# Summing the next stage's weights in quarter-width pieces beside the output product of a pooling layer

## The reference

```
x1 = x + (mix * silu(z)) @ w_out_a            # pooling layer's output, K = 2048, N = 1024
kv = rmsnorm(x1, norm_kv_g) @ w_kv            # shared keys and values
qz = rmsnorm(x1, norm_b_g) @ w_in_b           # queries and gate of the attention layer
```

## Time and profile before

| | |
|---|---|
| Time, median of 3 runs | 2968.87 us (2966.39 to 2971.01) |
| Time of the profiled execution | 2971.35 us |
| Its span, first to last instruction | 2969.7 us |
| TensorE busy | 2880.2 us, 97% |
| VectorE busy | 1802.3 us, 61% |
| ScalarE busy | 1401.6 us, 47% |
| DMA, mean over the span | 191 GB/s |
| TensorE's granted clock, mean | 0.991 of full speed |

### The profile page before, as it was taken

The page is one execution under the profiler, slowest core; times in us unless marked ns, Lnnn a source line. Parts: engine busy times, 40 slices in busy tenths (PEclk is TensorE's granted clock), DMA queues, the critical chain, the costliest instruction groups (busy, mean ns, idle before and its releaser), DMA issues. The chain is left out here.

```text
span 2969.7 us, 45966 instructions
## 1 busy us (share of the span) xinstructions
PE 2880.2 (97%) x17242; PEld 2418.4 (81%) x17242; DVE 1802.3 (61%) x2770; ACT 1401.6 (47%) x2232; POOL 128.4 (4%) x171
## 2 busy tenths in 40 slices
PE   8999999999989999999999999999999999988998
PEld 7888888888977887778888888889999999865787
DVE  3356556464443232376767666588888888644654
ACT  4444344342222222355646454377777777533322
POOL 0000000000000000000000000100000000022211
PEclk9999999999999999999999999999999999999999
DMA  7433433432526777698897878863544444399453
GB/s 254 161 116 121 155 120 116 156 123 100 197 74 216 243 247 244 230 302 288 274 300 253 274 259 252 259 159 86 114 101 111 101 110 117 131 416 405 160 187 107
DMA packets 326493, 567.27 MB, mean 191 GB/s; under 512 B 26761, under 2 KB 205561, under 8 KB 305689
## 3 DMA queue, kind: packets, MB, share of 16 engines
q1 hardware_dynamic: 324257, 564.61, 58.8%
q0 software_dynamic: 2048, 0.14, 0.0%
HBM read 424.69 MB, written 140.70 MB: 190 GB/s over the span
## 5 line engine op out<-in xcount | busy, mean ns | idle before, releaser
L2197 ACT ACTIVATE attn_scores<-attn_scores,attn_lowest 128x1024 f32<-128x1024 f32 (+15 forms) x256 | 306.7, 1202 | 2.7 <-DVE attn_lowest L2255 2.7
L2255 DVE CUSTOM_DVE_ANT_0 attn_scores<-attn_s,region_early 128x1024 f32<-128x1024 f32 (+7 forms) x256 | 216.7, 856 | 69.1 <-PE attn_s L2138 38.8
L268 PE MATMUL outa_acc<-outa_w_hi,outa_g_hi 128*128 128x512 f32 x512 | 203.9, 398 | 21.0 <-DVE outa_g_lo L1159 11.3
L268 PE MATMUL pool_acc<-pool_odd_x_hi,pool_wh 128*128 128x512 f32 (+1 forms) x640 | 223.2, 349 | 0.0
L270 PE MATMUL pool_acc<-pool_odd_x_hi,pool_wl 128*128 128x512 f32 (+1 forms) x640 | 222.9, 348 | 0.0
L269 PE MATMUL pool_acc<-pool_odd_x_lo,pool_wh 128*128 128x512 f32 (+1 forms) x640 | 222.9, 348 | 0.0
L269 PE MATMUL outa_acc<-outa_w_lo,outa_g_hi 128*128 128x512 f32 x512 | 202.2, 395 | 0.0
L270 PE MATMUL outa_acc<-outa_w_hi,outa_g_lo 128*128 128x512 f32 x512 | 201.7, 394 | 0.0
L268 PE MATMUL pool_acc<-even_x,pool_wh 128*128 128x512 f32 x512 | 200.1, 391 | 0.0
L270 PE MATMUL pool_acc<-even_x,pool_wl 128*128 128x512 f32 x512 | 199.3, 389 | 0.0
L269 PE MATMUL pool_acc<-even_x,pool_wh 128*128 128x512 f32 x512 | 199.2, 389 | 0.0
(11 more groups left out here) (364 smaller groups left out, 6962.7 us busy)
## 6 DMA issues: line engine op xcount, KB each, us to landing
region_early<-w_fold SPq DMA_DIRECT2D x110, 1024.0 KB, 6.9
pool_wz<-in_w_in_a SPq DMA_DIRECT2D x18, 2048.0 KB, 8.0
pool_wu<-w_mix SPq DMA_DIRECT2D x16, 2048.0 KB, 7.9
hold_kq<-in_cache_k SPq DMA_DIRECT2D x64, 512.0 KB, 6.9
region_early<-in_cache_v SPq DMA_DIRECT2D x60, 512.0 KB, 6.7
w_fold<-region_early SPq DMA_DIRECT2D x32, 896.0 KB, 5.6
region_early<-gatedT SPq DMA_DIRECT2D x16, 1024.0 KB, 7.8
gatedT<-pool_gates SPq DMA_DIRECT2D x48, 256.0 KB, 2.2
```

The source lines that it names most:

```text
L268: pe.matmul(out, ah, bh, start=first, stop=False)
L2197: act.activation(part, part, ACT.Exp, scale=-1.0, bias=low[s][:, x:x + 1], accum_out=sums[s][:, i:i + 1]).then_inc(expd, 1)
L2255: dve.tensor_tensor_reduce(sc[s][:, c, a0:a0 + n], s_ps[idx % 2][:, at0:at0 + n], bias[h % 2][:, b0:b0 + n], -SCALE, low[s][:, x - 2:x - 1 ...
```

## The change

Four things change. A place of an item holds 128 columns in place of 256, so that there are 64 items (`FN = 128`). They go round four slots in place of two (`NF = 4`), each with semaphores of its own. SP's load of the input rows moves from `step` to behind the items of the block (`next_x`). And on ScalarE and VectorE up to four items of a block are worked on ahead of the split (and on VectorE ahead of the add) that they followed before; the rest of the block's items stay behind it.

```diff
-        fold = [t[:, :, :].rearrange("p k n -> p (k n)")[:, 0:2048].rearrange("p (i n) -> p i n", i=8) for t in wst]
-        FN = 256
+        FN, NF = 128, 4
+        fold = [t[:, :, :].rearrange("p k n -> p (k n)")[:, h * 8 * FN:(h + 1) * 8 * FN].rearrange("p (i n) -> p i n", i=8)
+                for t in wst for h in range(2)]
...
-        fold_in, fold_out = ([m.sem(f"{n}{i}") for i in range(2)] for n in ("fold_in", "fold_out"))
+        fold_in, fold_out = ([m.sem(f"{n}{i}") for i in range(NF)] for n in ("fold_in", "fold_out"))
...
             def load_item(x):
                 kd, k, c = items[x]
                 _, w, half, _ = nxt.kinds[kd]
-                if x >= 2:
-                    sp.wait_ge(fold_out[x % 2], 16 * (x // 2))
+                if x >= NF:
+                    sp.wait_ge(fold_out[x % NF], 16 * (x // NF))
...
             def fold_items(b):
                 for x in items_of(b):
                     store_item(x)
-                    if x + 2 < len(items):
-                        load_item(x + 2)
-
-            def step(i, s, ahead, x_ahead):
+                    if x + NF < len(items):
+                        load_item(x + NF)
+
+            def step(i, s, ahead):
 
                 sp.wait_ge(added, 2 * i + s + 1)
                 dst = D["x1"][ds((2 * i + s) * P, P), :]
...
                 if ahead:
                     sp.wait_ge(g_lo, 2 * i + s + 3)
                     load_g(sp, 2 * i + s + 4, s, P)
-                if x_ahead:
-                    sp.wait_ge(out_sem[s], 16 * i + 16)
-                    load_x(2 * i + s + 2, s)
-
-            step(0, 0, True, True)
+
+            def next_x(b):
+                sp.wait_ge(out_sem[b % 2], 16 * (b // 2) + 16)
+                load_x(b + 2, b % 2)
+
+            step(0, 0, True)
             sp.wait_ge(w_lo, KC)
             sp.wait_ge(sample_mm, KC // LK)
-            load_item(0)
-            load_item(1)
-            step(0, 1, True, True)
+            for x in range(NF):
+                load_item(x)
+            next_x(0)
+            step(0, 1, True)
...
             for b in range(2, full - 2):
-                step(b // 2, b % 2, b + 4 < full, True)
+                step(b // 2, b % 2, b + 4 < full)
                 fold_items(b)
+                next_x(b)
...
             for b in range(2, full):
+                fold_items(items_of(b - 2)[:NF])
                 split(b // 2, b % 2)
-                fold_items(b - 2)
+                fold_items(items_of(b - 2)[NF:])
...
             for b in range(2, full - 2):
+                fold_items(items_of(b)[:NF])
                 add(b // 2, b % 2)
                 split(b // 2 + 1, b % 2)
-                fold_items(b)
+                fold_items(items_of(b)[NF:])
```

More of the change, by code:

```diff
@@ L1030, in load_item @@
                 _, w, half, _ = nxt.kinds[kd]
-                if x >= 2:
-                    sp.wait_ge(fold_out[x % 2], 16 * (x // 2))
+                if x >= NF:
+                    sp.wait_ge(fold_out[x % NF], 16 * (x // NF))
                 for r, at in ((k, slice(0, 8, 7)), (k + HK, slice(3, 7, 3))):
                     rows = w[r * P:(r + 1) * P, half * nxt.W:(half + 1) * nxt.W].rearrange("p (h n) -> p h n", h=2)
-                    sp.dma_start(fold[x % 2][:, at, :], rows[:, :, c * FN:(c + 1) * FN]).then_inc(fold_in[x % 2], 16)
+                    sp.dma_start(fold[x % NF][:, at, :], rows[:, :, c * FN:(c + 1) * FN]).then_inc(fold_in[x % NF], 16)
             def store_item(x):
@@ L1040, in store_item @@
                 at = k * HN + c * FN
-                sp.dma_start(D["w_fold"][kd].rearrange("i p n -> p i n")[:, :, at:at + FN], fold[x % 2][:, 0:7, :]
-                             ).then_inc(fold_out[x % 2], 16)
+                sp.dma_start(D["w_fold"][kd].rearrange("i p n -> p i n")[:, :, at:at + FN], fold[x % NF][:, 0:7, :]
+                             ).then_inc(fold_out[x % NF], 16)
             def fold_items(b):
@@ L1072, in on_sp @@
             fold_items(1)
+            next_x(1)
             for b in range(2, full - 2):
-                step(b // 2, b % 2, b + 4 < full, True)
+                step(b // 2, b % 2, b + 4 < full)
                 fold_items(b)
+                next_x(b)
                 if b == full - 4:
@@ L1080, in on_sp @@
                 sp.dma_start(first_rows[r], D["x1"][r * P:(r + 1) * P, :]).then_inc(row_sems[r], 16)
-            for s in range(2):
-                sp.wait_ge(fold_out[s], 16 * (len(items) // 2))
+            for out in fold_out:
+                sp.wait_ge(out, 16 * (len(items) // NF))
             nxt.load_raw(sp, 0)
             nxt.load_raw(sp, 1)
-            step(pairs - 1, 0, False, False)
+            step(pairs - 1, 0, False)
             sp.wait_ge(out_sem[0], 16 * pairs)
@@ L1089, in on_sp @@
             nxt.load_raw(sp, 2)
-            step(pairs - 1, 1, False, False)
+            step(pairs - 1, 1, False)
         self.mm, self.added, self.full = mm, added, full
@@ L1117, in on_act, with fold_items @@
                 act.activation(wh[:, k, :], wst[i % 2][:, r, :], ACT.Copy).then_inc(w_hi, 1)
-            def fold_items(b):
-                for x in items_of(b):
+            def fold_items(some):
+                for x in some:
                     kd, k, _ = items[x]
                     gain = gains[nxt.kinds[kd][3]]
-                    act.wait_ge(fold_in[x % 2], 32 * (x // 2) + 32)
+                    act.wait_ge(fold_in[x % NF], 32 * (x // NF) + 32)
                     for r, at in ((k, slice(0, 8, 7)), (k + HK, slice(3, 7, 3))):
-                        w = fold[x % 2][:, at, :]
+                        w = fold[x % NF][:, at, :]
                         act.activation(w, w, ACT.Copy, scale=gain[:, r:r + 1]).then_inc(fold_scaled, 1)
             for b in range(2, full):
+                fold_items(items_of(b - 2)[:NF])
                 split(b // 2, b % 2)
-                fold_items(b - 2)
+                fold_items(items_of(b - 2)[NF:])
             def row_square(r):
@@ L1175, in on_dve, with fold_items @@
                 dve.tensor_tensor(wl[:, k, :], wst[i % 2][:, r, :], f32(wh[:, k, :]), ALU.subtract).then_inc(w_lo, 1)
-            def fold_items(b):
-                for x in items_of(b):
-                    f = fold[x % 2]
+            def fold_items(some):
+                for x in some:
+                    f = fold[x % NF]
                     dve.wait_ge(fold_scaled, 2 * x + 2)
@@ L1191, in on_dve @@
             dve.tensor_tensor(xr[:, :], sample_acc[:, :], xr[:, :], ALU.add).then_inc(sample_added, 1)
-            fold_items(1)
+            fold_items(items_of(1))
             for b in range(2, full - 2):
+                fold_items(items_of(b)[:NF])
                 add(b // 2, b % 2)
                 split(b // 2 + 1, b % 2)
-                fold_items(b)
+                fold_items(items_of(b)[NF:])
             def row_average(r):
```

## The result

The changed kernel takes 3074.75 us (median of 5 runs, 3073.75 to 3079.51) against 2969.71 us before (median of 5, 2966.39 to 2973.65): a ratio of 1.0357, 95% interval 1.0344 to 1.0369, or 105 us slower. The forecast was 3111 us in a range of 3050 to 3165. The sign and the mechanism were right, the size too large by 36 us.

A forecast was written before the change was run, and what follows sets the result against it. SP's serial queue, already slower than TensorE, was taken as the bound: ten periods of 34.75 or 39.45 us put block 14's split 141.0 us later, plus 1 for clock, +142 on the median: 3111 us, range 3050 to 3165.

The forecast's parts named there:

- The bound: SP's queue in the nine blocks from 988.05: 24.4 us a block against TensorE's 22.0; shortening it earns at most some 11 us.
- n items cost n times c, whatever the slots: SP's queue: one store in the air despite four slots, 5.33 x 4.7 = 25.1 us a block against 16.8.
- The cycle c: SP's time for one item, two load issues 0.93 and a store landing 3.8: 4.7 us, range 3.8 to 5.1.
- The alternative estimate of 4.5 us: SP's time for one item, counting only what can't overlap: two load issues 0.93, then a store; some 4.5 us.
- rival 3: Fold items' DMAs: small packets run at full rate, an item takes 4.3 us, total 3092 us; chance 6%.
- The head wait: Block head: the split waits for the fourth item, loaded after the last store lands; 12.35 us, then 7.4 for g.
- The input rows: Block head: loading them behind the sums saves SP's 3.7 us x1-store wait and 0.5 MB before the first fold store.
- The clock: TensorE before the last two products: a restart after a 12 us gap at lower clock counts once, +1 us.
- The head wait is not hidden: Answers the rival that the fourth item's data come earlier: 8.55 us a block go, 94 in all, 3017 us; chance 4%.
- Small packets are cheaper than large ones: Answers the rival that 512 B store packets are no cheaper than 1 KB: 6.3 us an item, +77, 3188 us; chance 7%.
- doing nothing: Rival on the whole change: it does nothing, since the split is not late; chance 1%.
- rival 4: The change pays: SP's chain falls under 22.0 us a block and TensorE's waits go, 2956 us; chance 2%.

The follow-up runs named there:

- size_only: Kernel before with 128 columns in a place (64 items), still two slots and the old order everywhere: 3035.8 us, ratio 1.0223 to before.
- lag_no_ahead: no_ahead with SP loading item x + 3 behind the store of item x, so two stores are in the air: 2955.7 us, ratio 0.9954 to before.
- x_only: Kernel before with only the load of the input rows moved behind the items: 2972.5 us, ratio 1.0010 to before.
- no_ahead: Changed kernel with the sums behind the add and split again; small items, four slots and moved input rows stay: 3023.4 us, ratio 1.0184 to before.

## Why the prediction was right, and where its size was off

**The bound.** SP's serial chain was already slower than TensorE. Right: size_only shows it from one side, lag_no_ahead from the other, where TensorE's waits for the split vanish and 14.6 us are gained on the kernel before (the prediction's "at most some 11 us" left out the low clock behind the waits; TensorE is busy 3.9 us less).

**n items cost n times c, whatever the slots.** Right. 60 waits on the landing of the store just issued.

**The cycle c.** This is the step that was mis-sized: 4.7 us taken, 4.17 measured. The prediction had c 48 times in its sum, 48 x 0.53 = 25 us of the miss. Two numbers in it were wrong. I took 316 GB/s for small packets from a window of block loads, but the small fold stores run at 348 GB/s (first line, DMA view of the changed kernel, 1024.5 to 1025.3 us). The loads are no slower: while g is loaded, from 1013.5 to 1015.5 us, it is 346 (second line). The window of the earlier trace rows took in a slow start, 259 to 291 GB/s in its first ten slices against some 345 near its end.

```profile
DMA packets 545, 0.28 MB, mean 348 GB/s; under 512 B 1, under 2 KB 545, under 8 KB 545
DMA packets 1350, 0.69 MB, mean 346 GB/s; under 512 B 0, under 2 KB 1350, under 8 KB 1350
```

At 348 GB/s 0.72 MB are 2.07 us, which leaves 2.1 for the rest of the cycle, where I had taken 2.55 as independent of size; some of it, probably the ragged end of a store, shrinks with the item. The alternative estimate of 4.5 us, which counted only what can't overlap, was the better one, and the sum with c = 4.3 (rival 3) came nearest, at 3092 us. The Trainium skill ("DMA: Bandwidth & Descriptors", Specifications) says that 512 B is enough for line rate. The trace agrees in part: stores move 385 GB/s with 1 KB packets and 348 with 512 B, so the larger ones are 11% faster, and not the 22% that I took.

**The head wait.** Right in place and kind. Its terms, forecast and measured: last landing 3.8 and 3.35 (part of c), fourth item's loads 3.1 and 2.75, scalings 0.9 and 0.94, sums 1.05 and 0.94, add 1.2 and 1.13, split 2.3 and 2.28, g to the first landing 7.4 and 6.76. The load term makes 4 us of the miss over 11 blocks, the g term 7, sums and add 2. With 25 that is 38 us; the forecast of the median was 36 us too high, and the split of block 14 came 37.6 us earlier than forecast (1307.4 for 1345.0). TensorE's waits before blocks 4 to 14, forecast as 11 to 17 us each, are 7.1 to 12.1: SP's period is 31.6 us with five items in place of 34.75, and the product takes 23.7 us (1011.16 to 1042.86, less the wait of 8.02) in place of 22.0, at the lower clock.

**The input rows.** The claim that their gain "is real" was wrong for the reason shown in x_only: the wait was hidden behind the bytes that the same store has to follow. Between small-item kernels it is worth some 7 us in all, within the overlap of the intervals, not 3.7 a block. In the changed kernel the forecast was not hurt, since its head was summed from DMA data.

**The clock.** TensorE's lower clock after a wait, which I counted once, costs 20.6 us of busy time in all. It adds almost nothing to the end: the terms of SP's period add up to 31.6 us without one of TensorE's, so a slower product only shortens the next wait. Only behind the last wait could it count, and no run took that apart.

**The rivals.** The head wait is not hidden: without it (no_ahead) 51 us go. Small packets are cheaper than large ones, since c fell from 6.3 to 4.17. Full rate for small packets (rival 3) was nearer in c than my forecast, 4.3, but its reason holds only in part. Small items are not free, and the change is far from doing nothing. The faster case exists, at 2955.7 us where rival 4 named 2956, but by another edit: not by a shorter landing, but by not waiting for it.

## What to carry to other kernels

More buffers help only if the queue that fills them doesn't wait for the transfer it has just issued: look at what each wait names, and let it name the one before. Where a queue is serial, cutting pieces in half costs nearly the fixed part of a cycle for each new piece. Before work is put ahead of something that others wait for, ask which of its pieces arrives last, since that one sets the price; and before a wait is moved, ask which transfer the next step would wait for anyway.

## What the hardware showed that I had not expected

An instruction of SP that issues a DMA mostly takes 0.4 to 0.5 us, but the fold store's takes 5.54 to 6.32 us in ten blocks of x_only, where it stands right behind the input rows, the x1 store and g, and 3.90 to 5.04 with small items (no_ahead). This fits a queue that takes only so much before issuing itself blocks; how much it takes, in DMAs, packets or bytes, no run took apart.

Packets of 512 B move at 346 to 348 GB/s in loads and in stores alike, and packets of 1 KB in stores at 385.
